# An eleventh weight slot, a moved scatter, split last loads and a shared last norm in a two-layer mixture-of-experts trunk

## The chip, the core and the metric

The kernel runs on one core of one Trainium2 chip. The core has a matrix engine (TensorE, in the profile PE, its weight loads PEld), a vector engine (VectorE, DVE), an activation engine (ScalarE, ACT), GpSimd (POOL) and SyncE (SP), which here does nothing but start DMA transfers from memory into SBUF. The metric is the device time of one execution in microseconds (us), lower is better.

## What is computed

256 latent tokens and 256 context tokens of width 1024 pass through two layers. Layer 0 mixes tokens by differential attention, layer 1 by pooling over windows of 2, 4, 8 and 16 tokens. Behind each mixer comes a norm, then a mixture of 16 experts with two chosen for each token, then a second norm:

```python
def expert_block(args):
    xb, e = args
    return (jax.nn.silu(xb @ wg[e]) * (xb @ wu[e])) @ wd[e]
...
y2 = moe_ffn(tokens, router_w, router_b, moe_wg[i], moe_wu[i], moe_wd[i])
xl = deepnorm_update(xl, y2[:B * S].reshape(B, S, D), g2, ln_g[i, 1], ln_b[i, 1])
```

`deepnorm_update` is `layer_norm(ALPHA * x + (1 + gate) * y, g, b)`. The gates and shifts come from a product of the condition vector with `mod_w`, two times 1024 x 6144. Everything is float32. `wg`, `wu` and `wd` of one expert are three matrices of 1024 x 1024, 12.6 MB together, and all 32 experts are read once: 403 of the 480 MB that the program moves.

## The kernel before

The code is written out by hand for each engine, and semaphores tie the engines together. An engine works strictly through its own list.

**The ring.** Expert weights stream through `ring`, ten slots of 2 MB (128 partitions x 4096 floats). A unit is half a matrix, so an expert has six: 0 and 1 are `wg`, 2 and 3 `wu`, 4 and 5 `wd`. Unit number v counts through both layers; the small weights of the pooling mixer are a unit of their own between them (number 96), so the last unit is 192. SyncE sends unit v into slot `FREE[v % RING]` once TensorE has signalled `unit_used` for unit v - RING. The first ten units have conditions of their own in `slot_free`, since the slots still hold attention weights, q, k and v, or partial results then. The loads stand in one queue and land in order.

**The early part.** VectorE computes the condition products: 20 units of `mod_w` (here "sum units", in `LOADS` the bare numbers) come as halves of 1 MB into slots 2 and 3 by turns, and eight multiply-adds each sum them up (L1309), between the softmax steps of the attention. `LOADS` is the order in which SyncE sends all these.

**An expert.** At most 64 tokens per expert take part in the main path (a loop for further tokens, `further_experts`, follows each layer and is not entered with these inputs). TensorE multiplies the gathered tokens with the four units of `wg` and `wu` into PSUM banks 4 and 5 (`two_halves`, L887), gathers tokens of a coming pair of experts into bank 6 (`gather`, L879), waits until ScalarE and VectorE have made silu(a) * b (`h_ready`), turns that result (`turn_hidden`, L903), turns the routing weights of the next expert (L909), waits for the turned result to be copied to SBUF (`hTt_copied`, L1647), multiplies it with the two units of `wd` into bank 6, waits for VectorE to scale that with the gate into `ysb` (`ys_ready`, L1651), and adds it to the tokens' sums in banks 0 to 3 (`scatter`, L895). Banks 0 to 3 hold token tile t, half h in bank 2t + h until the layer ends.

**Small jobs.** `job` on TensorE and `job_out` on VectorE spread gates and other rows over partitions, one behind each of experts 1 to 6 of layer 0 (`LATE_JOB`). The last norm's gain rows are spread in layer 1's last two experts (`last_row`, L926) and copied by ScalarE into `joint`; its shift rows are spread behind the last scatter into banks 4 and 5.

**The last norm** (`last_norm`). VectorE waits for the whole last scatter and reads the count of further rounds. Then it takes statistics of the four banks (L1478), combines them for each tile (L1474), and makes two passes over each of the four 128 x 512 pieces: subtract the mean and multiply with the gain (L1537), then divide by the deviation and add the shift from PSUM (L1543). ScalarE makes only the two square roots. SyncE stores each piece when `out_ready` counts it.

## Time and profile before

| quantity | value |
|---|---|
| median of 3 runs (lowest, highest) | 1221.16 us (1218.96, 1221.24) |
| the profiled execution's own time | 1220.21 us |
| its span, first to last instruction | 1218.4 us |
| TensorE busy | 1130.0 us, 93% |
| VectorE, ScalarE, GpSimd busy | 357.8, 166.8, 5.2 us |
| moved by DMA | 480.17 MB, mean 394 GB/s |
| mean granted TensorE clock | 0.987 |

The profile is one execution. [...] A row of the timeline joins like instructions that follow each other, x64 for 64 of them; each product counts twice here, since a float32 product runs as two instructions. Idle time in front of an instruction stands in brackets, with what ended it. "DMA to landing" is the time from a transfer's issue to its arrival.

### The profile page before, as it was taken

To read this page: it belongs to the slowest core of one execution; us is meant where nothing else is said; L and a number is where in the kernel's file an instruction comes from. 1 tells how busy PE (TensorE), PEld (TensorE's weight loads), DVE (VectorE), ACT (ScalarE), POOL (GpSimd) and SP (SyncE) were. 2 spreads that over 40 slices of the span, in tenths; PEclk is the share of its full clock that TensorE was granted. 3 is DMA by queue.
4 is the path that set the end of the run, shared out by engine and by line. 5 is a ranking of instruction groups with operands and counts; after the bars stand their busy time and mean duration, and the time that the engine had idled before them with its cause. 6 is when DMAs were issued, how large, how long until landed. Compare 5 with 4: busy or idle time off the path is not lost.

```text
span 1218.4 us, 12360 instructions
## 1 busy us (share of the span) xinstructions
PE 1130.0 (93%) x5288; PEld 500.6 (41%) x5288; DVE 357.8 (29%) x729; ACT 166.8 (14%) x398; POOL 5.2 (0%) x8
## 2 busy tenths in 40 slices
PE   8998998899999999999999999999999999999995
PEld 3553554545344333333333337533333343333331
DVE  1559899763111211111111115211111111111113
ACT  1101233523000000000100006100000010000000
POOL 0000000000000000000000010000000000000000
PEclk9998999999999999999999999999999999999998
DMA  9998797984999999999999999899999999999993
GB/s 394 405 356 322 270 358 273 401 345 167 428 427 429 427 429 426 429 427 427 428 428 428 427 419 427 357 427 429 427 428 429 425 429 427 428 429 426 429 426 153
DMA packets 40153, 480.17 MB, mean 394 GB/s; under 512 B 5024, under 2 KB 6304, under 8 KB 8352
## 3 DMA queue, kind: packets, MB, share of 16 engines
q1 hardware_dynamic: 39040, 476.91, 93.9%
q10 hardware_dynamic: 1056, 2.43, 0.6%
q8 instruction: 44, 0.72, 0.2%
q14 instruction: 13, 0.11, 0.0%
HBM read 476.18 MB, written 1.05 MB: 392 GB/s over the span
## 4 chain that ended last, share of the span: by engine, by line
PE 82%; DVE 9%; DMA 6%; issue 2%; ACT 1%; DVEq 0%; ACTq 0%
PE ps L887 53%; PE ps L879 5%; PE ps L895 5%; DMA ring<-in_moe_wu 3%; PE ps L638 3%; DMA ring<-in_mod_w 3%; PE ps L738 2%; PE ps L641 2%; DVE work L1647 2%; DVE work L1651 1%; DVE ring L1309 1%; PE ps L903 1%; PE ps L579 1%; PE ps L701 1%; PE ps L644 1%
## 5 line engine op out<-in xcount | busy, mean ns | idle before, releaser
L887 PE MATMUL ps<-ring,tra 128*64 128x512 f32 x2048 | 446.7, 594 | 1.0 <-DMA ring<-in_moe_wu 1.0
L887 PEld LDWEIGHTS ps<-ring,tra 128*64 128x64 f32 x2048 | 144.1, 137 | 298.4 <-issue 295.7
L887 PE MATMUL ps<-ring,work 128*64 128x512 f32 x1024 | 228.7, 598 | 29.2 <-DVE work L1647 29.2
L887 PEld LDWEIGHTS ps<-ring,work 128*64 128x64 f32 x1024 | 83.2, 137 | 154.1 <-issue 117.3
L1642 DVE TENSOR_TENSOR work<-ps,work 128x512 f32<-128x512 f32 x32 | 22.1, 692 | 277.2 <-ACT work L1198 277.2
L1198 ACT ACTIVATE work<-ps 128x512 f32<-128x512 f32 x32 | 19.1, 597 | 533.5 <-PE ps L887 533.5
L895 PE MATMUL ps<-work,extra 64*128 64x512 f32 x256 | 63.6, 615 | 21.0 <-DVE work L1651 21.0
L1191 ACT ACTIVATE tra<-ps,cols 128x128 f32<-128x128 f32 x128 | 48.1, 456 | 240.2 <-PE ps L879 240.2
L1645 DVE TENSOR_TENSOR work<-work,ps 128x512 f32<-128x512 f32 x32 | 22.0, 689 | 181.7 <-PE ps L887 181.7
L879 PEld LDWEIGHTS ps<-extra,xn 128*128 128x128 f32 x512 | 61.0, 195 | 24.3 <-issue 22.7
L879 PE MATMUL ps<-extra,xn 128*128 128x128 f32 x512 | 66.9, 285 | 1.4 <-DVE extra L1555 1.4
L638 PE MATMUL ps<-ring 128*128 128x512 f32 x128 | 58.5, 612 | 0.7 <-ACT ring L1073 0.7
L895 PEld LDWEIGHTS ps<-work,extra 64*128 64x128 f32 x256 | 22.0, 186 | 61.4 <-DVE work L1651 46.3
L1651 DVE TENSOR_TENSOR work<-ps,gt 128x512 f32<-128x512 f32 x16 | 11.1, 691 | 116.9 <-PE ps L887 116.9
L1651 DVE TENSOR_TENSOR work<-ps,rows 128x512 f32<-128x512 f32 x16 | 11.1, 691 | 115.5 <-PE ps L887 115.5
L1309 DVE SCALAR_TENSOR_TENSOR ring<-ring,cols 128x512 f32<-128x512 f32 x56 | 42.1, 752 | 3.2 <-DMA ring<-in_mod_w 1.2
L638 PEld LDWEIGHTS ps<-ring 128*128 128x128 f32 x128 | 24.5, 196 | 33.9 <-issue 33.8
L1647 DVE COPY work<-ps 128x512 f32<-128x512 f32 x32 | 22.2, 692 | 50.0 <-PE ps L903 50.0
L1309 DVE SCALAR_TENSOR_TENSOR extra<-ring,cols,extra 128x512 f32<-128x512 f32 x42 | 31.6, 752 | 2.2 <-DMA ring<-in_mod_w 0.7
L1309 DVE SCALAR_TENSOR_TENSOR modp<-ring,cols,modp 128x512 f32<-128x512 f32 x42 | 31.6, 752 | 1.5
L579 PE MATMUL ps<-cst 128*128 128x512 f32 x44 | 24.6, 691 | 4.2 <-DMA cst<-in_consts 4.0
L644 PE MATMUL ps<-ring 128*128 128x256 f32 x128 | 28.4, 380 | 0.0
(184 smaller groups left out, 712.4 us busy)
## 6 DMA issues: line engine op xcount, KB each, us to landing
ring<-in_moe_wg SPq DMA_DIRECT2D x64, 2048.0 KB, 23.9
ring<-in_moe_wu SPq DMA_DIRECT2D x64, 2048.0 KB, 23.4
ring<-in_moe_wd SPq DMA_DIRECT2D x64, 2048.0 KB, 23.0
ring<-in_mod_w SPq DMA_DIRECT2D x40, 1024.0 KB, 9.7
ring<-in_mod_w SPq DMA_DIRECT2D x4, 2048.0 KB, 18.5
ring<-in_attn_wqkv SPq DMA_DIRECT2D x4, 2048.0 KB, 11.2
ring<-in_attn_wo SPq DMA_DIRECT2D x2, 2048.0 KB, 10.9
ring<-in_tokens SPq DMA_DIRECT2D x2, 1024.0 KB, 16.3
```

Source lines behind the costliest of these rows:

```text
L579: mm(bank(bk), ident, cst[:, 0:NB], start=True, stop=True, skip_group_check=True)
L638: return mm(bank(acc_bank(g)), w[:, k, t * P:t * P + P], hT[:, k, :], start=first, stop=end)
L641: return mm(bank(acc_bank(g)), hT[:, k, t * P:t * P + P], rhs, start=first, stop=end)
L644: last = mm(bank(acc_bank(g), 0, P, n * TOK, (n + 1) * TOK), w[:, k, hd * P:hd * P + P], hT[:, k, 0:TOK], start=first and n == 0, stop=end ...
L738: last = mm(bank(2 * t + h), oT[t][:, k, :], wo[:, k, :], start=(k == 0), stop=(k == KT - 1))
L879: last = mm(bank(bk, 0, P, k * P, k * P + slots), xn[:, c0:c0 + P], sgat[:, t, 0:slots], start=(t == 0), stop=(t == TT - 1), skip_group_ch ...
L887: last = mm(ps[SLOTS * h:SLOTS * h + SLOTS, b, :], lhs(k0 + k), w[:, k, h * NB:(h + 1) * NB], start=(k0 + k == 0), stop=(k0 + k == KT - 1) ...
L895: last = mm(bank(2 * t + h), sw[SLOTS * h:SLOTS * h + SLOTS, t * P:t * P + P], ysb[SLOTS * h:SLOTS * h + SLOTS, :], start=False, stop=True ...
L1191: nc.scalar.activation(xg[i // 2 % 2][:, kk, :], bank(bk, k * P, k * P + P), ACT.Identity, bias=one(bcol[2 * layer], kk, 1), scale=one(aco ...
L1309: ins = v_.scalar_tensor_tensor(out=acc, in0=w[:, k, :], scalar=ck, in1=acc, op0=ALU.mult, op1=ALU.add)
L1647: v_.tensor_copy(work[:, NB:2 * NB], bank(7)).then_inc(sem("hTt_copied"), 1)
L1651: v_.tensor_tensor(ysb, bank(6), gt[layer], ALU.mult).then_inc(sem("ys_ready"), 1)
```

## The change

Four edits, named here in the order of the program.

1. The ring has eleven slots (`RING = 11`). The room in SBUF comes from a smaller scratch area for DMA descriptors that GpSimd would write, which this program doesn't use (`dynamic_dma_scratch_size=128`). Slot 10 is new and first in `FREE`. `AHEAD = 1`: unit 0 of layer 0 goes there without a condition, in the list `LOADS` behind sum unit 9. All other early units keep their slot and condition under a number higher by one.
2. TensorE's scatter of expert e no longer stands behind its down product but in the next expert, behind the turning of its hidden result. The last expert of each layer keeps a scatter of its own at the end.
3. Units 3 and 5 of the very last expert are sent as two loads of 1 MB with a semaphore each (`LAST_UNITS`, `last_unit`), and TensorE multiplies each half when it is there.
4. The last norm: gain and shift rows are spread as jobs behind experts 1 to 4 of layer 1 and copied to SBUF by VectorE (`joint`, `lnb`); the last scatter signals each bank (`summed`), and VectorE starts its statistics bank by bank; piece (tile 0, half 1) is made by ScalarE (subtract and divide) and GpSimd (multiply, add), and the stores go in another order.

```diff
-RING = 10
-FREE = (4, 8, 5, 9, 6, 7, 2, 3, 1, 0)
+RING = 11
+FREE = (10, 4, 8, 5, 9, 6, 7, 2, 3, 1, 0)
+LAST_UNITS = tuple(LAYER_BASE[1] + (NE - 1) * EU + n for n in (3, 5))
...
-LATE_JOB = {e: EARLY_JOBS + e - 1 for e in range(1, 7)}
+LATE_JOB = {(0, e): EARLY_JOBS + e - 1 for e in range(1, 7)} | {(1, e): EARLY_JOBS + 5 + e for e in range(1, 5)}
...
+                if v in LAST_UNITS:
+                    load(to[:, 0:2], of[:, 0:2], sem(f"last_first_{n}"))
+                    load(to[:, 2:4], of[:, 2:4], sem(f"ring_loaded_{s}"))
+                else:
+                    load(to, of, sem(f"ring_loaded_{s}"))
...
+            z = xn[:, NB:D]
+            pool.wait_ge(sem("job_out"), len(JOBS))
+            pool.wait_ge(sem("last_scaled"), 1)
+            nc.gpsimd.tensor_tensor(z, z, joint[:, NB:D], ALU.mult).then_inc(sem("last_weighed"), 1)
+            pool.wait_ge(sem("last_weighed"), 1)
+            nc.gpsimd.tensor_tensor(z, z, lnb[1], ALU.add).then_inc(sem("pool_out"), 1)
...
+            def last_unit(b, lhs, v, n, k0):
+
+                w = slot(ring_slot(v)[0]).rearrange("p (k n) -> p k n", k=4)
+                pe.wait_ge(sem(f"last_first_{n}"), 16)
+                two_halves(b, lhs, w, k0, range(2))
+                landed(pe, v)
+                return two_halves(b, lhs, w, k0, range(2, 4))
...
+                if e:
+                    pe.wait_ge(sem("ys_ready"), q)
                 if pr_ + 1 < PAIRS:
                     pe.wait_ge(sem("sgat_ready"), PAIRS * layer + pr_ + 2)
                     gather(6, e2).then_inc(sem("gather_done"), 1)
...
                 turn_hidden().then_inc(sem("hT_turned"), 1)
+                if e:
+                    scatter(swT[(e - 1) % 2]).then_inc(sem("scattered"), 1)
...
-                pe.wait_ge(sem("ys_ready"), q + 1)
-                scatter(swT[e % 2]).then_inc(sem("scattered"), 1)
+                if q == DEPTH * NE - 1:
+                    pe.wait_ge(sem("ys_ready"), q + 1)
+                    scatter(swT[e % 2], sem("summed")).then_inc(sem("summed"), 1)
+                elif e == NE - 1:
+                    pe.wait_ge(sem("ys_ready"), q + 1)
+                    scatter(swT[e % 2]).then_inc(sem("scattered"), 1)
...
             std(3, 0)
+            act.wait_ge(sem("last_shift"), 1)
+            nc.scalar.activation(xn[:, NB:D], bank(1), ACT.Identity, bias=mv[:, 4:5], scale=mv[:, 2:3])\
+                .then_inc(sem("last_scaled"), 1)
             std(3, 1)
...
+                dve.wait_ge(sem("job_out"), len(JOBS))
+                for h in range(2):
+                    half_stats(0, h)
+                spread(n, 0)
+                half_stats(1, 0)
+                dve.wait_ge(sem("std_ready"), TT * n + 1)
+                link(v_.reciprocal(mv[:, 2:3], mv[:, 3:4]))
+                v_.scalar_tensor_tensor(out=mv[:, 4:5], in0=mv[:, 0:1], scalar=-1.0, in1=mv[:, 2:3], op0=ALU.mult,
+                                        op1=ALU.mult).then_inc(sem("last_shift"), 1)
+                half_stats(1, 1)
+                spread(n, 1)
+                weighed(0, 0)
+                dve.wait_ge(sem("var_ready"), TT * n + 2)
+                for h in range(2):
+                    weighed(1, h)
```

SyncE's list in the early part, before, from sum unit 9 (the second row of `in_mod_w` begins with it) to the first expert units (`in_moe_wg`):

```order
L418 DMA ring<-in_attn_wqkv 128x4096 [waits unit_used]
L418 DMA ring<-in_mod_w 128x2048 [waits half_summed] x8
L418 DMA ring<-in_attn_wqkv 128x4096 [waits unit_used]
L418 DMA ring<-in_mod_w 128x2048 [waits half_summed] x4
L418 DMA ring<-in_attn_wo 128x4096 [waits unit_used]
L418 DMA ring<-in_mod_w 128x2048 [waits half_summed] x6
L418 DMA ring<-in_attn_wo 128x4096 [waits unit_used]
L418 DMA xn<-in_x 128x2x1024
L418 DMA ring<-in_mod_w 128x2048 [waits half_summed] x4
L418 DMA ring<-in_moe_wg 128x4096 [waits unit_used]
```

And now:

```order
L422 DMA ring<-in_mod_w 128x2048 [waits half_summed] x2
L422 DMA ring<-in_moe_wg 128x4096
L422 DMA ring<-in_mod_w 128x2048 [waits half_summed] x6
L422 DMA ring<-in_attn_wqkv 128x4096 [waits unit_used]
L422 DMA ring<-in_mod_w 128x2048 [waits half_summed] x4
L422 DMA ring<-in_attn_wo 128x4096 [waits unit_used]
L422 DMA ring<-in_mod_w 128x2048 [waits half_summed] x6
L422 DMA ring<-in_attn_wo 128x4096 [waits unit_used]
L422 DMA xn<-in_x 128x2x1024
L422 DMA ring<-in_mod_w 128x2048 [waits half_summed] x4
L422 DMA ring<-in_moe_wg 128x4096 [waits unit_used]
```

The load of 2 MB without a wait stands behind the two halves of sum unit 9; the six halves of units 10 to 12 follow it, and the first unit with a condition (`unit_used`) stands where unit 0 stood.

TensorE in layer 1, an expert with an even number, from the turning of the next weights to the next expert's first unit (`ring_loaded_` and a slot number), before:

```order
L909 MATMUL ps<-cst,extra 128x128 [waits ssc_ready]
L909 MATMUL ps<-cst,extra 128x128
L887 MATMUL ps<-ring,work 64x512 [waits ring_loaded_0,xg_copied,hTt_copied]
L887 MATMUL ps<-ring,work 64x512 x7
L887 MATMUL ps<-ring,work 64x512 [waits ring_loaded_4]
L887 MATMUL ps<-ring,work 64x512 x7
L895 MATMUL ps<-work,extra 128x512 [waits ys_ready]
L895 MATMUL ps<-work,extra 128x512 x3
L887 MATMUL ps<-ring,tra 64x512 [waits ring_loaded_8,swT_copied,xg_copied]
```

And now, from the gather of such an expert on (`L931` is the turning, `L921` the scatter):

```order
L905 MATMUL ps<-extra,xn 128x128 [waits sgat_ready,ys_ready]
L905 MATMUL ps<-extra,xn 128x128 x7
L931 MATMUL ps<-cst,work 128x128 [waits h_ready]
L931 MATMUL ps<-cst,work 128x128 x3
L921 MATMUL ps<-work,extra 128x512 x4
L937 MATMUL ps<-cst,extra 128x128 [waits ssc_ready]
L937 MATMUL ps<-cst,extra 128x128
L913 MATMUL ps<-ring,work 64x512 [waits ring_loaded_5,xg_copied,hTt_copied]
L913 MATMUL ps<-ring,work 64x512 x7
L913 MATMUL ps<-ring,work 64x512 [waits ring_loaded_9]
L913 MATMUL ps<-ring,work 64x512 x7
L913 MATMUL ps<-ring,tra 64x512 [waits ring_loaded_6,swT_copied,xg_copied]
```

The scatter has lost its wait for `ys_ready` (the gather, which writes the same bank, has it), and stands between the turning and the down product that waits for `hTt_copied`; the next expert's first unit stands directly behind the down product.

VectorE in the last norm, before:

```order
L1478 BN_STATS stat<-ps 128x6
L1478 BN_STATS stat<-ps 128x6 [waits dve_chain]
L1474 BN_AGGR mv<-stat 128x2 [waits dve_chain]
L1478 BN_STATS stat<-ps 128x6
L1478 BN_STATS stat<-ps 128x6 [waits dve_chain]
L1474 BN_AGGR mv<-stat 128x2 [waits dve_chain]
L1537 SCALAR_TENSOR_TENSOR xn<-ps,mv,modp 128x512 [waits lng_copied,var_ready]
L1541 RECIPROCAL mv<-mv 128x1 [waits std_ready,dve_chain]
L1543 SCALAR_TENSOR_TENSOR xn<-xn,mv,ps 128x512 [waits lnb_spread,dve_chain]
```

And now:

```order
L1521 BN_STATS stat<-ps 128x6 [waits summed,job_out]
L1521 BN_STATS stat<-ps 128x6 [waits summed,dve_chain]
L1517 BN_AGGR mv<-stat 128x2 [waits dve_chain]
L1521 BN_STATS stat<-ps 128x6 [waits summed]
L1590 RECIPROCAL mv<-mv 128x1 [waits std_ready,dve_chain]
L1591 SCALAR_TENSOR_TENSOR mv<-mv 128x1 [waits dve_chain]
L1521 BN_STATS stat<-ps 128x6 [waits summed]
L1517 BN_AGGR mv<-stat 128x2 [waits dve_chain]
L1576 SCALAR_TENSOR_TENSOR xn<-ps,mv,modp 128x512
L1581 SCALAR_TENSOR_TENSOR xn<-xn,mv,pscale 128x512 [waits dve_chain]
```

Each statistic waits for its own bank's sum, two small instructions for ScalarE's share stand between them, and the second pass reads its shift from `pscale` in SBUF where it read `ps`.

## Rows read from the trace of the kernel before

**Rows 1.** Windows of core 0: stretch, length, busy by engine, PEclk, DMA share, GB/s

```profile
275.00:291.00 16.00, 14.65 (x112) 10.99 (x106) 8.01 (x41) 9.01 (x20) 0.00 (x0) 0.98 0.00 0
292.00:765.00 473.00, 444.98 (x2230) 192.50 (x2227) 85.57 (x215) 51.21 (x108) 4.96 (x4) 1.00 1.01 426
765.00:775.00 10.00, 10.00 (x54) 5.80 (x55) 1.68 (x7) 3.01 (x8) 0.00 (x0) 0.89 0.57 212
```

**Rows 2.** Timeline of the end: start, length, engine, line, count, idle before and releaser

```profile
1184.65 0.42 PEld L887 LDWEIGHTS ps<-ring,tra 128*64 128x64 f32 x4 [0.44 <-DMA ring<-in_moe_wu]
...
1189.55 0.20 PEld L887 LDWEIGHTS ps<-ring,tra 128*64 128x64 f32 x4 [1.91 <-DMA ring<-in_moe_wu]
...
1195.60 7.34 PE L887 MATMUL ps<-ring,work 128*64 128x512 f32 x32 [0.79 <-DVE work L1647]
...
1199.29 0.20 PEld L887 LDWEIGHTS ps<-ring,work 128*64 128x64 f32 x4 [0.92 <-DMA ring<-in_moe_wd]
...
1203.74 1.99 PE L895 MATMUL ps<-work,extra 64*128 64x512 f32 x8 [0.80 <-DVE work L1651]
...
1206.63 1.43 DVE L1478 BATCH_NORM_STATS2 stat<-ps 128x6 f32<-128x512 f32 x2 [2.95 <-PE ps L895]
...
1215.24 0.75 DVE L1543 SCALAR_TENSOR_TENSOR xn<-xn,mv,ps 128x512 f32<-128x512 f32 x1
```

**Rows 3.** TensorE timeline, first units of two successive experts in layer 1

```profile
1124.48 13.95 PE L887 MATMUL ps<-ring,tra 128*64 128x512 f32 x64
...
1151.85 0.65 PE L887 MATMUL ps<-ring,tra 128*64 128x512 f32 x2
```

**Rows 4.** Single ring loads on SyncE: issue time, and time from issue to landing

```profile
L418 SPq DMA_DIRECT2D ring<-in_moe_wd x1: 328/328/328, 680.3 to 680.3; - x1
DMA to landing us min/median/max: 37.6/37.6/37.6
...
L418 SPq DMA_DIRECT2D ring<-in_moe_wu x1: 328/328/328, 748.0 to 748.0; - x1
DMA to landing us min/median/max: 24.4/24.4/24.4
...
L418 SPq DMA_DIRECT2D ring<-in_moe_wd x1: 328/328/328, 772.4 to 772.4; - x1
DMA to landing us min/median/max: 7.9/7.9/7.9
```

**Rows 5.** Timeline and windows, last expert of layer 0, and one window later

```profile
714.17 0.74 PE L903 MATMUL ps<-cst,work 128*128 128x128 f32 x4 [0.86 <-DVE work L1645]
...
715.70 8.78 PE L887 MATMUL ps<-ring,work 128*64 128x512 f32 x32 [0.79 <-DVE work L1647]
...
724.53 0.69 DVE L1651 TENSOR_TENSOR work<-ps,gt 128x512 f32<-128x512 f32 x1 [8.89 <-PE ps L887]
...
716.10:719.50 3.40, 3.40 (x10) 0.98 (x8) 0.00 (x0) 0.00 (x0) 0.00 (x0) 0.50 1.06 383
...
1187.10:1190.50 3.40, 2.37 (x14) 0.64 (x12) 0.00 (x0) 0.00 (x0) 0.00 (x0) 1.00 1.00 419
```

**Rows 6.** Second half of sum unit 9 on SyncE, and VectorE at unit 10

```profile
L418 SPq DMA_DIRECT2D ring<-in_mod_w x1: 328/328/328, 109.5 to 109.5; - x1
DMA to landing us min/median/max: 8.8/8.8/8.8
...
127.58 0.48 DVE L1307 TENSOR_SCALAR modp<-ring,cols 128x512 f32<-128x512 f32 x1
```

**Rows 7.** Waits of TensorE: who waited for whom: us in total, times, longest

```profile
PE ps L887 <- DVE work L1647: 29.2, 32, 0.9
...
PE ps L895 <- DVE work L1651: 21.0, 27, 0.8
```

**Rows 8.** Groups of instructions: ScalarE from PSUM, and GpSimd's products

```profile
L1198 ACT ACTIVATE work<-ps 128x512 f32<-128x512 f32 x32 | 19.1, 597 | 533.5 <-PE ps L887 533.5
...
L541 POOL TENSOR_TENSOR ring<-ring,modp 128x512 f32<-128x512 f32 x4 | 5.0, 1270 | 720.5 <-DMA ring<-in_pool_w 720.5
```

More of the change, by code:

```diff
@@ L469, in _ @@
                     load_rows()
+                elif what == "ahead":
+                    for n in range(AHEAD):
+                        load_unit(0, 0, n)
                 elif what == "x":
@@ L768, in job @@
                     last = columns_of(bk, rows[1], 1, NMOD, 4 * NMOD)
+                elif kind in ("lng", "lnb"):
+                    last = mm(bank(bk), pick((10 if kind == "lng" else 18) + int(n)), rows[0][:, :], start=True, stop=True)
                 elif kind == "joint":
@@ L889, in two_halves, with scatter @@
                 return last
-            def scatter(sw):
+            def scatter(sw, each=None):
                 for t in range(TT):
@@ L896, in scatter @@
                                   ysb[SLOTS * h:SLOTS * h + SLOTS, :], start=False, stop=True, skip_group_check=True)
+                        if each is not None and (t, h) != (TT - 1, 1):
+                            last.then_inc(each, 1)
                 return last
@@ L1682, in body @@
                     v_.tensor_tensor(ysb, bank(6), gt[layer], ALU.mult).then_inc(sem(x_ + "ys"), 1)
[L1683 to L1684 removed]
+                scattered = lambda: dve.wait_ge(*((sem("scattered"), NE) if layer == 0 else (sem("summed"), 2 * TT)))
+                if layer == 0:
+                    scattered()
+                further(dve, layer, chunk, body, first=scattered if layer else None,
+                        end=lambda: dve.wait_ge(sem("further_done"), layer + 1))
             def pool_layer():
```

153 lines of the change are left out of this document (75 added, 78 removed).

## The prediction

> **What bounds the kernel now.** I read the shares of the page first: TensorE is busy 93% of the span, and the core moves 394 GB/s on average. The windows say where the rest of the stream is. Between 275 and 291 us the queues move nothing, from 292 to 765 they run at 426 GB/s, and from 765 to 775 there is a second hole [rows 1]. The reader is to see two machines: TensorE, which looks busy, and the weight stream, which from 292 us on stops nowhere else.
>
> Which of the two ends last? One expert is 12.6 MB in six units. Where TensorE waits for loads, units come 4.90 us apart (1189.55 - 1184.65) [rows 2], so the stream needs 29.4 us for an expert. TensorE starts an expert every 27.37 us (1151.85 - 1124.48) [rows 3]. TensorE is the faster one and eats up the lead that a full ring gives the stream, 2.0 us per expert. In layer 0 the lead just suffices: the last unit lands at 680.3 + 37.6 = 717.9 [rows 4], and TensorE, which has begun the last two units at 715.70, doesn't wait for it [rows 5]. In layer 1 it doesn't suffice: the last units are waited for, the last until 1199.29, and from there to the end of the span it is 19.1 us [rows 2]. The end of the kernel is thus the end of the weight stream plus a tail.
>
> **The ring and the early load.** What fills a hole in the stream brings all later loads forward; bytes stay the same. The first hole arises because all ten slots are full at 275 and the first is released at 291. Every old unit keeps its condition, shifted by one number, and the new unit 0 goes to slot 10, which nobody uses earlier. So at 291 one unit more is on board and every later unit lands one place, 4.90 us, earlier. This is paid where unit 0 is sent, behind sum unit 9: that half is issued at 109.5 and lands at 118.3 (109.5 + 8.8) [rows 6]. With 4.9 us more the queue is at 123.2, the first half of sum unit 10 (1 MB, half of 4.9) lands at about 125.7, and VectorE takes it at 127.58 [rows 6]. So it costs nothing, with 1.9 us to spare; if the cover were gone, VectorE's sums, and with them all that follows, would be up to 4.9 us late.
>
> The second hole: the load issued at 748.0 lands at 772.4 (24.4), the next is issued only at 772.4, when the first unit of layer 1 has been multiplied, and lands 7.9 us later [rows 4]. Units follow at 4.9 otherwise, so 3.0 us are lost. After the change one more unit may be loaded before this release, and the stream is one unit ahead: the queue is busy until the same 772.4. The release itself comes earlier (next part, by 7.2 us, at 765.2); issued 7.2 us before the queue ends, the load has no hole before it. Gain 3.0. The last unit then lands at 1199.3 - 4.9 - 3.0 = 1191.4.
>
> **The scatter behind the next turning.** TensorE's wait for the scaled result before each scatter (21.0 us in 27 waits, 0.78 each) and its wait for the copied turning (29.2 in 32, 0.91 each) are both covered now [rows 7]; by the single rows they are 0.8 and 0.95, so an expert falls from 27.37 to about 25.6 us. I cost this at nearly nothing although it is 16 x 1.7 = 28 us per layer. Left to itself TensorE would end layer 0 some 26 us before 724.5, at about 698, but the last unit lands only at 717.9 - 4.9 = 713.0. What hides the gain is the stream. It shows only at the two layer ends. In layer 0 before, the last pair of units ran from 715.70 to 724.53 [rows 5]. Now the end is set by unit 3 of expert 15, which lands at 713.0 - 9.8 = 703.2: 3.65 for its products (a quarter of the 13.95 of four units [rows 3], and 0.15 to their end), 0.9 to the turning, and from the turning's start to the down product 1.5 (715.70 - 714.17) [rows 5] plus 0.9, since the scatter (1.99, of which the old wait covers about 1.1) stands there now, then twice the products, 7.1. That gives 717.3, 7.2 earlier. All of the layer boundary moves with it.
>
> **The tail.** In layer 1 the units 3 and 5 of the last expert come as two halves. Unit 2 lands at 1191.4 - 14.7 = 1176.7 and takes 3.65; unit 3, half of it early, ends at 1183.9; 0.9 to the turning, 2.4 to the down product, 7.1 for it: 1194.3, which is 2.9 after the last landing, against 3.7 before (1202.94 - 1199.29) [rows 2]. From there 0.8 to the scatter, as before (1203.74 - 1202.94).
>
> From the scatter's start to VectorE's last end it was 1215.99 - 1203.74 = 12.25 [rows 2]. VectorE began 2.9 after the scatter's start and can now begin after a quarter of it, about 0.7: -2.2. Two of its eight passes of 0.75, at 0.71 apart, go to ScalarE and GpSimd: -1.4. Two [128x1] instructions more in the chain: +0.1. The spreading products leave TensorE's end, where nobody waited long for them. So 8.75. The side branch: ScalarE (0.60) and twice GpSimd (1.27 each) [rows 8] from about 3.5 give 6.9, before VectorE's end, so its store is no bound. The stores' own 2.4 stay.
>
> **Sum.** The last landing -7.9, products behind it -0.8, norm -3.5: 12.2 off the span of 1218.4, so 1206.2, and with the 1.8 that lie around it in the profiled execution (1220.2) 1208.0. The median of the runs is 0.95 above that execution, 1221.2, so by the median it would be 1209.0; I say 1208.3. Bounds: the ring between 4.9 and 0 (early load in the way); second hole 3.0 to 0; scatter's added time in the last expert 0 to 1.99; VectorE's start 0.5 to 1.0 after the scatter's; the GpSimd branch 1.27 to 2 x 1.27 per pass, the longer one giving 9.4 and 0.7 more. The four loads of 1 MB in place of two of 2 MB: nothing to 0.4 us more; I take nothing, since no row sets the two sizes apart.
>
> **GpSimd beside VectorE.** No row shows a VectorE instruction with both inputs in SBUF beside a GpSimd instruction. The nearest is the scaling at 724.53, with one input in PSUM, which ran 0.69 beside GpSimd's four [rows 5, 8], the mean of its kind; so the sum above takes 0, and the bound is that each of two passes waits out one GpSimd pass, 2 x 1.27. [...]
>
> **Rivals.**
> [...]
> - *The early load is in the way*: sum unit 10 late, all later by up to 4.9: 1213.2. Against it the 1.9 us of margin.
> - *The boundary doesn't come earlier* (a wait in layer 0's last expert that I don't see): the hole of 3.0 stays in part: 1211.
> - *The loads don't move, only the tail does*: 1221.2 - 4.3 = 1216.9. It needs a stream that slows when more units are outstanding; but the load that took 37.6 us to land [rows 4] stood behind seven others at 4.9 each.
> [...]
> - *TensorE is the bound after all*: 32 x 1.7 = 54 faster, 1167. It needs loads closer than 4.90; no row has them.
>
> **How the numbers follow.** Forecast (both holes filled, shorter tail, no lock) 0.46, with the lock 0.30, early load in the way 0.08, boundary 0.05, tail alone 0.06, slower clock 0.04, TensorE bound 0.01. Within 0.2% (2.4 us, about what a measurement of this kernel can tell from none) lies half of the tail-alone case. Faster 0.93, same 0.03, slower 0.04. The range from 1205.2 (no scatter in the last turning, VectorE starting at 0.5, and 1 us as two executions differ) to 1212.2 (lock and one slow stretch at the end, or part of a hole left) holds the first two cases and most of the fourth.
>
> **What the profile after would show.** No unit's landing later than one unit earlier from 300 on; windows without a hole at 765 to 775 and with 11 to 12 us of nothing in place of 16 before 291; waits of TensorE for loads in the last third of each layer, no waits for the scaled result; first statistics 0.7 after the last scatter's start, not 2.9. Wrong would be: sum unit 10 waited for, GpSimd's second pass ending behind VectorE's last, a clock of 0.50 in many windows, or units further apart than 4.9.

## The result and the profile after

The changed kernel takes 1204.05 us (median of 4 runs, 1203.59 to 1207.20), the kernel before beside it 1220.06 us (median of 4, 1218.74 to 1221.24). The ratio is 0.9865, with a 95% interval from 0.9847 to 0.9882: 16.0 us less, where 12.2 were forecast as a sum. The profiled execution took 1203.59 us with a span of 1201.6, against 1220.21 and 1218.4, so its span is 16.8 us shorter.

The page of the changed kernel: busy times with shares of the span, and the chain that ended last.

```profile
span 1201.6 us, 12396 instructions
...
PE 1134.2 (94%) x5288; PEld 494.0 (41%) x5288; DVE 362.4 (30%) x732; ACT 166.6 (14%) x397; POOL 8.0 (1%) x10
...
PE 69%; DMA 23%; DVE 6%; ACT 1%; issue 1%; another core or an unknown queue 0%; DVEq 0%; SPq 0%; ACTq 0%
```

TensorE is no less busy than before. 23% of the chain is now waiting for DMA.

The windows that answer to [rows 1], with one ahead of the first hole and one at the end (columns as there, times in us from the span's start; PEclk is the granted clock as a share of TensorE's full speed):

```profile
208.00:276.00 68.00, 60.42 (x256) 33.02 (x260) 46.04 (x91) 27.83 (x74) 0.00 (x0) 0.91 0.89 361
276.00:292.00 16.00, 14.67 (x110) 11.01 (x104) 8.01 (x41) 9.02 (x20) 0.00 (x0) 0.96 0.00 0
292.00:760.00 468.00, 450.35 (x2254) 192.03 (x2250) 87.29 (x216) 52.78 (x112) 4.94 (x4) 0.99 1.01 428
...
765.00:775.00 10.00, 10.00 (x50) 3.57 (x47) 1.20 (x2) 0.60 (x1) 0.00 (x0) 1.00 1.01 418
...
775.00:1180.00 405.00, 388.68 (x1877) 150.16 (x1877) 61.93 (x133) 31.54 (x73) 0.00 (x0) 1.00 1.01 430
```

Three things are to be seen. The second hole is gone (418 GB/s from 765 to 775, against 212). The first hole is as long as it was, 16 us of nothing. And the stream runs faster between the holes: 428 where it was 426, though both stretches hold slower pieces. An undisturbed stretch of both kernels shows it better. First before, then after:

```profile
800.00:1150.00 350.00, 327.51 (x1616) 132.62 (x1612) 50.37 (x114) 27.31 (x65) 0.00 (x0) 1.00 1.01 427
```

```profile
800.00:1150.00 350.00, 338.90 (x1638) 129.86 (x1636) 54.06 (x118) 27.36 (x65) 0.00 (x0) 1.00 1.01 431
```

That is 0.9% more bytes in the same time. By the landings of single units in the trace, the median step from one 2 MB unit to the next fell from 4.894 to 4.848 us. Of the packets of 16 KB, 29% took 611 ns before, with a median of 613 and 13% at 620 or more; now 97% take 611. Between 800 and 1150 the mean packet took 616.0 ns before and takes 612.2 now.

The single loads that answer to [rows 4, 6] (issue time, then the time to landing):

```profile
L422 SPq DMA_DIRECT2D ring<-in_moe_wg x1: 433/433/433, 109.9 to 109.9; - x1
...
DMA to landing us min/median/max: 14.4/14.4/14.4
...
L422 SPq DMA_DIRECT2D ring<-in_moe_wd x1: 328/328/328, 292.1 to 292.1; - x1
...
DMA to landing us min/median/max: 8.7/8.7/8.7
...
L422 SPq DMA_DIRECT2D ring<-in_moe_wd x1: 328/328/328, 764.1 to 764.1; - x1
...
DMA to landing us min/median/max: 10.2/10.2/10.2
...
L422 SPq DMA_DIRECT2D ring<-in_moe_wd x1: 4215/4215/4215, 1145.6 to 1145.6; - x1
...
DMA to landing us min/median/max: 40.2/40.2/40.2
```

The early load lands at 124.3 and is in nobody's way. The load released at 764.1 has to queue (10.2 us, where 7.9 was a load without a queue). The last unit lands at 1145.6 + 40.2 = 1185.8, 13.45 earlier than the 1199.25 of before.

The timeline of the tail, which answers to [rows 2]:

```profile
1166.13 3.65 PE L913 MATMUL ps<-ring,tra 128*64 128x512 f32 x16 [1.12 <-DMA ring<-in_moe_wg]
...
1171.00 7.09 PE L913 MATMUL ps<-ring,tra 128*64 128x512 f32 x32 [1.21 <-DMA ring<-in_moe_wu]
...
1181.61 7.09 PE L913 MATMUL ps<-ring,work 128*64 128x512 f32 x32
...
1188.74 0.69 DVE L1705 TENSOR_TENSOR work<-ps,rows 128x512 f32<-128x512 f32 x1 [8.25 <-PE ps L913]
...
1189.49 1.99 PE L921 MATMUL ps<-work,extra 64*128 64x512 f32 x8 [0.79 <-DVE work L1705]
...
1190.72 1.43 DVE L1521 BATCH_NORM_STATS2 stat<-ps 128x6 f32<-128x512 f32 x2 [1.28 <-PE ps L921]
...
1194.12 0.70 DVE L1576 SCALAR_TENSOR_TENSOR xn<-ps,mv,modp 128x512 f32<-128x512 f32 x1
...
1194.30 1.26 POOL L563 TENSOR_TENSOR xn<-xn,modp 128x512 f32<-128x512 f32 x1 [475.42 <-ACT xn L1285]
1194.85 1.27 DVE L1581 SCALAR_TENSOR_TENSOR xn<-xn,mv,pscale 128x512 f32<-128x512 f32 x1
1195.64 1.59 POOL L565 TENSOR_TENSOR xn<-xn,gt 128x512 f32<-128x512 f32 x1
...
1198.48 0.75 DVE L1581 SCALAR_TENSOR_TENSOR xn<-xn,mv,gt 128x512 f32<-128x512 f32 x1
```

The down product ends at 1188.70, 2.9 behind the last landing (3.7 before). VectorE starts 1.23 after the scatter and ends at 1199.23, 9.74 after the scatter's start (12.25 before). One second pass takes 1.27 in place of 0.75, beside GpSimd.

So the span's 16.8 us are 13.45 at the last landing, 0.8 in the products and 2.5 in the norm. If the forecast's two terms hold, the landing's part is one unit (4.85) and the second hole (3.0), less 1.0, since the stream restarts later after the first hole in this execution (the load lands at 300.74 and not at 299.71); the 6.6 that remain would be the pace, for which the forecast had no term. The experiments measure each of the three. What remained to be found out was whether the pace belongs to the program, and which edit brought it.

### The profile page after: what moved, and what is told of

The parts are those of the page before. It is cut to its first block, busy times and chain, and to the rows that moved or that the text cites. A ratio compares the mean times of both kernels' runs of the same rounds, so it can differ in the third digit from the quotient of the medians.

```text
span 1201.6 us, 12396 instructions
## 1 busy us (share of the span) xinstructions
PE 1134.2 (94%) x5288; PEld 494.0 (41%) x5288; DVE 362.4 (30%) x732; ACT 166.6 (14%) x397; POOL 8.0 (1%) x10
## 4 chain that ended last, share of the span: by engine, by line
PE 69%; DMA 23%; DVE 6%; ACT 1%; issue 1%; another core or an unknown queue 0%; DVEq 0%; SPq 0%; ACTq 0%
PE ps L913 41%; DMA ring<-in_moe_wu 12%; DMA ring<-in_moe_wg 8%; PE ps L905 4%; PE ps L921 4%; DMA ring<-in_mod_w 3%; PE ps L662 3%; PE ps L762 2%; PE ps L665 2%; DVE ring L1350 1%; PE ps L725 1%; PE ps L668 1%; PE ps L743 1%; DVE modp L1350 1%; PE ps L578 1%; PE ps L931 1%
## 5 line engine op out<-in xcount | busy, mean ns | idle before, releaser
L913 PE MATMUL ps<-ring,tra 128*64 128x512 f32 x2048 | 454.1, 597 | 24.2 <-DMA ring<-in_moe_wu 19.2
L913 PEld LDWEIGHTS ps<-ring,tra 128*64 128x64 f32 x2048 | 147.5, 138 | 322.6 <-issue 280.8
L913 PEld LDWEIGHTS ps<-ring,work 128*64 128x64 f32 x1024 | 71.6, 137 | 135.6 <-issue 133.3
L921 PE MATMUL ps<-work,extra 64*128 64x512 f32 x256 | 63.6, 615 | 1.6 <-DVE work L1705 1.6
L921 PEld LDWEIGHTS ps<-work,extra 64*128 64x128 f32 x256 | 22.0, 186 | 22.1 <-issue 15.1
L1684 DVE COPY extra<-ps 128x256 f32<-128x256 f32 x32 | 13.6, 424 | 48.4 <-PE ps L937 48.4
```

What stands on the lines that cost most here:

```text
L913: last = mm(ps[SLOTS * h:SLOTS * h + SLOTS, b, :], lhs(k0 + k), w[:, k, h * NB:(h + 1) * NB], start=(k0 + k == 0), stop=(k0 + k == KT - 1) ...
L921: last = mm(bank(2 * t + h), sw[SLOTS * h:SLOTS * h + SLOTS, t * P:t * P + P], ysb[SLOTS * h:SLOTS * h + SLOTS, :], start=False, stop=True ...
```

## The experiments

In each, "before" is the kernel before on the same chip. The first four take the ring and the pace apart.

**1. The kernel before, unchanged, once more.**

> The kernel before, unchanged, on the chip on which the next three run. In the two profiles at hand a unit of 2 MB took 4.895 us in the kernel before and 4.845 in the changed one, already for the loads before 100 us that both send alike. If this pace belongs to the chip or the day, this run has the same pace as the changed kernel on this chip. If it belongs to the program (where its slots lie in SBUF, or the room kept for descriptors), it stays at 4.90 here and the changed kernel at 4.85. Time: equal to itself, within 0.2%.

Measured: 1220.03 us against 1220.56, ratio 0.9997 (0.9987 to 1.0006); units 4.895 us apart. So the pace is no matter of the chip or of the moment.

**2. The small scratch alone.** The change also reserves 128 bytes for the DMA scratch in place of the default 16 KB, to make room for the eleventh slot.

```diff
-    nc = bacc.Bacc("TRN2", target_bir_lowering=False, num_devices=1)
+    nc = bacc.Bacc("TRN2", target_bir_lowering=False, num_devices=1, dynamic_dma_scratch_size=128)
```

> Before, with only the scratch for descriptors cut from 16 KB to 128 bytes for each partition, so that every tile lies some 16 KB lower. If the place in SBUF or the scratch sets the pace of the loads, units land 4.85 apart here against 4.90 in the run beside it, and the end comes 1 to 2.5 us earlier, which is what TensorE waits for loads at the end of layer 1. If not, no change: 0 us, pace as in the run beside it.

Measured: 1217.78 us against 1220.56, ratio 0.9974 (0.9965 to 0.9983). Units come 4.848 us apart and the last lands at 1196.25, 3.0 earlier; TensorE waits for no load at all, and its down product ends only 1.5 earlier, at 1201.46. 97% of the 16 KB packets take 611 ns. This one edit brings the pace. Its down product follows VectorE's copy and no load:

```profile
1194.38 7.09 PE L887 MATMUL ps<-ring,work 128*64 128x512 f32 x32 [0.78 <-DVE work L1647]
```

**3. The ring and the early load, with the small scratch.**

```diff
-RING = 10
-FREE = (4, 8, 5, 9, 6, 7, 2, 3, 1, 0)
+RING = 11
+FREE = (10, 4, 8, 5, 9, 6, 7, 2, 3, 1, 0)
...
+LOADS = [... ("q", 1), 9, "ahead", 10, 11, 12, ("v", 1), 13, 14,
...
+AHEAD = 1
...
+    nc = bacc.Bacc("TRN2", target_bir_lowering=False, num_devices=1, dynamic_dma_scratch_size=128)
```

> Before, with the eleventh slot and the early load of unit 0 and the small scratch, the rest as it was. Mine: the stream is one unit (4.9 us) ahead, but TensorE is then the bound at 27.37 us per expert through both layers; only its waits for loads in the last expert go, 1.5 to 2.5 us faster. The rival, that loads moved forward pay by themselves, gives 5 to 8 us faster. If the early load were in the way of sum unit 10, the start of the experts (287.5) would be up to 5 us later and the time not better.

Measured: 1218.34 us against 1220.56, ratio 0.9981 (0.9972 to 0.9990): no better than the scratch alone. The last unit lands another 1.7 earlier (1194.55) although this profile's experts began 3.4 later than in the kernel before, at 290.9, after stretches of a lower granted clock (0.80 from 276 to 291, against 1.00); nobody profits, because TensorE, without a wait for a load, needs until 1204.78.

**4. The changed kernel once more.**

> The changed kernel, unchanged, on the same chip as the first three: again some 16 us faster than the kernel before. Its pace of loads beside that of the first run tells whether the 5.6 us that my sum lacked up to the last landing come from the program or from the chip: with equal paces the gap to the kernel before would be 11 to 12 us here, with 4.90 against 4.85 it stays at 16.

Measured: 1204.80 us, ratio 0.9870 (0.9855 to 0.9885), units 4.855 apart, last landing 1186.39.

The next two take the scatter.

**5. The moved scatter alone.**

```diff
+                if e:
+                    pe.wait_ge(sem("ys_ready"), q)
...
                 turn_hidden().then_inc(sem("hT_turned"), 1)
+                if e:
+                    scatter(swT[(e - 1) % 2]).then_inc(sem("scattered"), 1)
...
-                pe.wait_ge(sem("ys_ready"), q + 1)
-                scatter(swT[e % 2]).then_inc(sem("scattered"), 1)
+                if e == NE - 1:
+                    pe.wait_ge(sem("ys_ready"), q + 1)
+                    scatter(swT[e % 2]).then_inc(sem("scattered"), 1)
```

> Before, with only the scatter moved behind the next expert's turning (ten slots, full scratch). Mine: each expert of TensorE falls from 27.37 to about 25.6 us where units are there, but the stream ends where it did, so layer 0 ends 2 us earlier, the second hole shrinks by that much, and the kernel is 1.5 to 2.5 us faster. The rival, that TensorE's saved waits count (32 x 1.7), gives up to 54 us faster.

Measured: 1219.0 us against 1220.94, ratio 0.9992 (0.9983 to 1.0001), so between nothing and 2 us. In the profile layer 0 ends 1.6 earlier (722.9), the second hole closes (4.90 us between the two landings there, where it was 7.88) and the last landing is 2.5 earlier (1196.78), at 4.896 a unit; TensorE now waits 42.5 us for loads, where it waited 1.0.

**6. The changed kernel with the scatter in its old place.** The diff is the reverse of the last, but the very last scatter keeps its signal for each bank.

> The changed kernel with the scatter back in its old place, all else kept (eleven slots, halves, last norm, small scratch). If ring and scatter pay only together, this is TensorE at 27.37 us per expert through both layers and the time is that of the ring alone less about 2.6 for the last norm, 1215.5 to 1216.5, so that undoing the scatter costs 11 us. If the parts add up, it costs only the 2 us of the run with the scatter alone, 1206.5.

Measured: 1216.21 us against 1220.94, ratio 0.9962 (0.9949 to 0.9976). Undoing an edit that is worth 1 to 2 us alone costs 11 to 12. Its timeline at the end and its window at the second hole:

```profile
1194.96 0.69 DVE L1697 COPY work<-ps 128x512 f32<-128x512 f32 x1 [0.84 <-PE ps L931]
1195.71 7.09 PE L913 MATMUL ps<-ring,work 128*64 128x512 f32 x32 [0.78 <-DVE work L1697]
...
765.00:775.00 10.00, 10.00 (x54) 6.17 (x55) 1.68 (x7) 3.01 (x8) 0.00 (x0) 0.85 0.26 88
```

The last unit has landed at 1191.97, but the down product starts at 1195.71, released by VectorE's copy and by no load: TensorE is the bound. The faster stream only makes the second hole deeper (88 GB/s where it was 212), since TensorE frees the next slot at 773 as ever. From the first expert of layer 1 to its down product's end TensorE takes 433.5 us here without a wait for a load (769.3 to 1202.8). The kernel before took 434.2 (768.7 to 1202.95). So before the change the two bounds stood close together at the end, 1.5 us apart by the profile of experiment 2. Speeding up one alone gave 2.8 us by the medians (2.1 to 4.3) for the stream and 1.9 (0 to 2.1) for TensorE, with the eleventh slot on top of the quick stream nothing more; both together give the 16.

The next seven say what sets the pace. Each was executed once and agrees with the kernel before in its time to within what single executions differ by, so what counts is the pace in its trace and not its time.

**7. The small scratch with every tile at its old address.**

```diff
+        sb("pad", 4064)
         ring = sb("ring", RING * UNIT)
...
+    nc = bacc.Bacc("TRN2", target_bir_lowering=False, num_devices=1, dynamic_dma_scratch_size=128)
```

> Before, with the scratch of 128 bytes and a dead tile of 16256 bytes in front of the ring, so that every tile lies where it lies in the kernel before. If the place of the tiles sets the pace, units land 4.895 us apart as in the kernel before; if the scratch does, 4.848 as in the run with the small scratch. Time 1218 to 1221 either way.

Measured: 1223.79 us in one run (its experts began at 291.2 and not at 287.5, so 3.7 us of it are the early part), units 4.895 apart, and 29% of the 16 KB packets took 611 ns, as in the kernel before. The same scratch with the tiles moved gave 4.848 and 97% (experiment 2). It isn't the scratch, it is where the tiles lie.

Where is that? My expectations give every address 128 too low. The ring is the kernel's first tile, but ahead of it stand the scratch and 128 bytes of constants that the allocation itself puts there: its next free byte before the first tile is 16481 with the default scratch and 225 with the small one, and a tile begins at the next multiple of 32. So the ring begins at byte 16512 of each partition with the default scratch, and at byte 256 with the small one; in this experiment the unused tile of 16256 bytes begins at 256, and the ring at 16512 as in the kernel before. The sizes agree: with 256 unused bytes ahead of the ring and the default scratch, the allocation has reached byte 229344 before the last small tile, which is 16384 + 128 + 256 and 212576 for the tiles between. The titles below have the true addresses.

**8. The default scratch, and 128 unused bytes ahead of the ring,** which puts it at byte 16640.

```diff
+        sb("pad", 32)
         ring = sb("ring", RING * UNIT)
```

> The kernel before with an unused tile of 128 bytes per partition ahead of the ring, default scratch: the ring begins at byte 16512 of a partition and not at 16384 (with the small scratch it begins at 128). Theory A (what counts is where a slot begins within some power of two, and 128 bytes off is what the changed kernel has): loads every 4.848 us, nearly all 16 KB packets 611 ns, time 1216.5 to 1219. Theory B (what counts is the absolute place, the lower 16 KB being the quicker, or the total distance of 16 KB): loads every 4.895 us, packets spread from 611 to 622 ns, time 1219 to 1224.

Measured: 1218.89 us in one run, units 4.853 apart, 97% of the 16 KB packets at 611 ns. So 128 bytes are enough. The window of an undisturbed stretch:

```profile
800.00:1150.00 350.00, 327.66 (x1614) 132.54 (x1610) 50.09 (x113) 27.31 (x65) 0.00 (x0) 1.00 1.01 431
```

**9. The ring at byte 16576.** As the last, with `sb("pad", 16)`.

> The kernel before with an unused tile of 64 bytes ahead of the ring, which then begins at byte 16448 of a partition (257 x 64). Theory A (only a ring on a multiple of 16 KB is slow): loads every 4.85 us, packets 611 ns. Theory B (a multiple of 128 bytes that is not one of 16 KB is what is quick, and 64 off is not enough or costs more): 4.89 or longer, packets above 611 ns. Time 1216 to 1220 under A.

Measured: 1219.77 us in one run, units 4.894 apart; only 14% of the 16 KB packets took 611 ns, 46% 613 and 19% 620. Theory A fell; B stood until experiments 10, 11 and 13.

**10. The ring at byte 2176.** Small scratch and `sb("pad", 480)`.

> The kernel before with the 128-byte scratch and an unused tile of 1920 bytes: the ring begins at byte 2048. Theory A (only multiples of 16 KB are slow): loads every 4.85 us. Theory C (any multiple of 2 KB or more is slow): every 4.89 us, packets from 611 to 622 ns.

Measured: 1222.88 us in one run (experts from 290 on), units 4.893 apart. The pace is the one that Theory C gives, but at 2176 the ring is on no multiple of 2 KB, so its reason falls too.

```profile
800.00:1150.00 350.00, 328.29 (x1620) 132.98 (x1618) 49.56 (x112) 27.31 (x65) 0.00 (x0) 1.00 1.01 428
```

**11. The ring at byte 8320.** Small scratch and `sb("pad", 2016)`.

> The kernel before with the 128-byte scratch and an unused tile of 8064 bytes: the ring begins at byte 8192. Theory A (only multiples of 16 KB are slow): loads every 4.85 us. Theory C (a large power of two is slow): every 4.89 us. If 2048 is quick and 8192 slow, the bound lies between.

Measured: 1220.09 us in one run, units 4.895 apart. As in the last, the pace of Theory C without its reason.

**12. The ring at byte 16512 as before, all other tiles 128 bytes on.** `sb("pad", 32)` behind the ring.

> The kernel before with an unused tile of 128 bytes behind the ring, default scratch: the ring stays at byte 16384, every other tile lies 128 bytes further on. Theory (what counts is the address that a load writes to, so the ring): expert units every 4.89 us, 16 KB packets from 611 to 622 ns, time 1219 to 1224. Rival (it is the place of the tiles that the engines work in, beside which the loads write): 4.85 us, 611 ns, 1217 to 1219.

Measured: 1220.75 us in one run, units 4.894 apart, 30% of the packets at 611 ns. Moving the other tiles by these 128 bytes does nothing; moving the ring with them (experiment 8) does all.

**13. The ring at byte 384.** Small scratch and `sb("pad", 32)`.

> The kernel before with the 128-byte scratch and an unused tile of 128 bytes ahead of the ring: the ring begins at byte 256 of a partition. Theory A (odd multiples of 128 bytes are quick, even ones slow): expert units every 4.89 us, packets from 611 to 622 ns, time 1219 to 1224. Theory B (any small multiple of 128 bytes past a multiple of 2 KB is quick): 4.85 us, 611 ns, time 1216 to 1219.

Measured: 1219.63 us in one run, units 4.895 apart.

```profile
800.00:1150.00 350.00, 327.53 (x1614) 132.64 (x1612) 50.77 (x115) 27.34 (x65) 0.00 (x0) 1.00 1.01 428
```

Theory A foresaw the pace, but with 128 added to each address its rule turns round. Of the seven places tried, 256 and 16640, both multiples of 256, are quick; 384, 2176, 8320 and 16512, odd multiples of 128, and 16576, an odd multiple of 64, are slow. Slots are 16 KB per partition, so all of them share the ring's offset. All seven fit one rule: a slot that begins on a multiple of 256 bytes is quick. Two quick places are few, both are odd multiples of 256, and a ring at byte 512 was not run. An eighth place, byte 16768 (256 unused bytes, default scratch), has no result: the tiles don't fit in SBUF any more.

The next three undo parts of the change in the kernel in which the stream is the bound.

**14. The changed kernel with ten slots and without the early load,** small scratch kept.

```diff
-RING = 11
-FREE = (10, 4, 8, 5, 9, 6, 7, 2, 3, 1, 0)
+RING = 10
+FREE = (4, 8, 5, 9, 6, 7, 2, 3, 1, 0)
...
-AHEAD = 1
+AHEAD = 0
...
```

The conditions in `slot_free` go back by one number with it.

> The changed kernel with ten ring slots again and without the early load; the 128-byte scratch stays. Theory (the stream bounds, and the forecast's ring terms of 4.9 and 3.0 were right): 2 MB loads land every 4.85 us as in the changed kernel, the last one near 1193.7 (1185.8 + 7.9), and the time is 1212.3 (1211.5 to 1213.5). Rival 1 (the pace comes with the eleventh slot): loads every 4.895, last landing near 1200, time about 1218.5. Rival 2 (the ring gives nothing once the scatter is moved, as it gave nothing to the kernel before beyond the small scratch): time within 1.5 us of 1204.5.

Measured: 1209.08 us against 1220.24, ratio 0.9913 (0.9896 to 0.9929). Last landing 1190.78. The slot is worth 5.0 us, and not the 7.9 that I expected: of the second hole only a rest comes back with ten slots, so it was the moved scatter that had filled most of it.

```profile
765.00:775.00 10.00, 10.00 (x48) 3.30 (x46) 0.69 (x1) 0.60 (x1) 0.00 (x0) 1.00 0.92 365
```

The rest is 1.3 us: at 774.6 a unit lands 6.18 after the one before it, where a step is 4.85. At the quick pace the stream reaches this place earlier, so its hole is larger than before: in experiment 2 the same step is 11.61.

**15. As the last, and the default scratch too.**

> As the run above, and the scratch back at its default, so that every tile is at its old address: what is left of the change is the moved scatter, the halved last units and the last norm. Theory (place of the tiles): loads every 4.895 us, last landing near 1200 (1193.7 + 6.6), time 1218.7 less the small part that layer ends absorb, so 1217.5 to 1219.5. Rival (the small scratch is worth only the 2.5 us that it gave to the kernel before): 1214.5 to 1215.5. The tail behind the last landing should be 3.3 us shorter than before in either (1.6 is the forecast's 0.8 + 2.55 for the norm by the changed kernel's trace).

Measured: 1215.29 us against 1220.24, ratio 0.9964 (0.9950 to 0.9978); units 4.896 apart, last landing 1196.59. The place of the ring is worth 6.2 us here (1215.29 to 1209.08; 5.8 by the last landings), against 2.8 in the kernel before. My expectation of 1217.5 to 1219.5 was too high, because it brought back a hole that the scatter fills. The rival's range is met, but not for its reason: it put the place at 2.5 on top of a slot of 7.9. The tail behind the last landing is 16.0 us, 3.1 shorter than before, where 3.3 were expected.

**16. The changed kernel, eleven slots, unit 0 sent behind the sum units.**

```diff
-LOADS = [... ("q", 1), 9, "ahead", 10, 11, 12, ("v", 1), 13, 14,
+LOADS = [... ("q", 1), 9, 10, 11, 12, ("v", 1), 13, 14,
...
-AHEAD = 1
+AHEAD = 0
...
-                if v < AHEAD:
+                if v == 0:
                     return
```

> The changed kernel with eleven slots, but the first expert unit sent after the sum units and not ahead of sum unit 10. Theory (one unit fetched early is one unit step less at the end): last landing near 1190.6 (1185.8 + 4.85), time 1209.3 (1208.3 to 1210.3). Rival (the early load pushed the restart of the stream back by 1.0, which comes back when it is gone): last landing 1189.6, time 1208.3. Rival 2 (the stretch in which it was sent was free of consequence because TensorE is late anyway): no change, 1204.5.

Measured: 1204.0 us against 1220.24, ratio 0.9872 (0.9855 to 0.9888), the same as the changed kernel; last landing 1184.34. The early load gives nothing. Its window where the first units are loaded:

```profile
208.00:276.00 68.00, 59.35 (x260) 31.77 (x260) 46.23 (x92) 28.24 (x76) 0.00 (x0) 0.95 0.94 394
276.00:291.00 15.00, 14.24 (x100) 11.03 (x102) 8.00 (x41) 8.51 (x19) 0.00 (x0) 1.00 0.00 0
```

Between 208 and 276 the changed kernel moved 361 GB/s, since loads there wait for slots that the attention still holds. Unit 0, with its own slot, finds room in that stretch (394 GB/s), and eleven units are on board before the hole either way, the last of them at 274.1 here and at 276.0 in the changed kernel.

**17. VectorE reads the last norm's shift from PSUM again.**

```diff
+            for h in range(2):
+                mm(bank(4 + h), pick(18 + h), rows[0][:, :], start=True, stop=True).then_inc(sem("lnb_spread"), 1)
...
-                    v_.scalar_tensor_tensor(out=z, in0=z, scalar=m_[:, 2:3], in1=lnb[h], op0=ALU.mult,
+                    dve.wait_ge(sem("lnb_spread"), h + 1)
+                    v_.scalar_tensor_tensor(out=z, in0=z, scalar=m_[:, 2:3], in1=bank(4 + h), op0=ALU.mult,
```

> The changed kernel, but VectorE's second passes of the last norm take the shift row from PSUM banks 4 and 5, as before the change (TensorE spreads it again behind the last scatter), GpSimd's still from SBUF. If VectorE and GpSimd lock each other out when VectorE has two inputs in SBUF, the second pass of the first piece falls from 1.27 to 0.75 us, GpSimd's add from 1.59 to about 1.27, and the end comes about 1.0 us earlier. If the length came from something else, nothing changes.

Measured: 1203.34 us against 1220.94, ratio 0.9860 (0.9844 to 0.9875). Its timeline:

```profile
1188.82 1.99 PE L921 MATMUL ps<-work,extra 64*128 64x512 f32 x8 [0.79 <-DVE work L1708]
...
1193.63 1.27 POOL L563 TENSOR_TENSOR xn<-xn,modp 128x512 f32<-128x512 f32 x1 [475.63 <-ACT xn L1287]
1194.18 0.75 DVE L1584 SCALAR_TENSOR_TENSOR xn<-xn,mv,ps 128x512 f32<-128x512 f32 x1
...
1194.98 1.26 POOL L565 TENSOR_TENSOR xn<-xn,gt 128x512 f32<-128x512 f32 x1
...
1197.26 0.75 DVE L1584 SCALAR_TENSOR_TENSOR xn<-xn,mv,ps 128x512 f32<-128x512 f32 x1
```

The same pass, still beside GpSimd, takes 0.75 and not 1.27, which is also what the changed kernel's last pass takes with two inputs in SBUF when GpSimd is done (1198.48). GpSimd's second product takes 1.26 and not 1.59, and VectorE ends 9.19 after the scatter's start and not 9.74: reading the shift from SBUF costs 0.55 us. The median is 0.7 below the changed kernel's, which is less than these runs can tell for sure.

**18. Both: no early load, shift from PSUM.**

> The changed kernel without the early load (unit 0 is sent behind the sum units) and with the shift of the last norm read from PSUM by VectorE. Theory: both changes keep their single results, 0 from the first and about 0.6 to 1 us from the second, so 1203.3 (1202.5 to 1204.3), the same as the run with the PSUM shift alone. Rival (the early load delays the restart of the stream by up to 1 us, as the landings say): 1202.3.

Measured: 1203.32 us (5 runs, 1201.98 to 1206.01) against 1220.3, ratio 0.9861 (0.9842 to 0.9881). As the last; the early load can be left out. The rival falls: without the early load the stream restarts as late as in the changed kernel (first landing at 300.63). By the medians these two versions are the fastest that I ran.

**The edits in one row.** By medians: before 1220.2; the scatter alone 1219.0; with the tail too (experiment 15) 1215.3; with the ring at byte 256 (14) 1209.1; with the eleventh slot (16) 1204.0; with the early load, the changed kernel, 1204.05 to 1204.8. So 1 to 2, 3.7, 6.2, 5.1 and 0.

The same steps by the landings, from the first behind the first hole to the last, without the tail:

| kernel | first, last landing | between |
|---|---|---|
| before | 299.71, 1199.25 | 899.5 |
| scatter and tail (15) | 299.81, 1196.59 | 896.8 |
| and the ring at byte 256 (14) | 299.36, 1190.78 | 891.4 |
| and the eleventh slot (the changed kernel) | 300.74, 1185.80 | 885.1 |

The scatter brings 2.8; the place 5.4, which is a pace of 6.7 less the 1.3 of the hole that ten slots leave (experiment 2, whose stretch is 896.6 with a hole of 6.8, against 899.5 with one of 3.0, gives the same 6.7 for the pace); the slot 6.4, the unit of 4.85, this 1.3, and 0.2 left over. Together 14.5, less the later restart 13.45.

## Why the prediction missed

The direction and the mechanism were right, and the time came 4.3 us below the forecast and 1.15 below the range. The step that failed is the price of a unit: "Units follow at 4.9 otherwise", with "bytes stay the same", from which the last landing came forward by 4.9 and 3.0 only. The last-landing term was 7.9 and measured 13.45; 6.6 to 6.7 of it are the pace of 4.848 us (the table above), by experiments 2, 7, 8 and 12 an effect of where the ring lies. The line of the diff that makes the scratch small was in front of me, and I read it as making room and took its price for nothing. The rival "TensorE is the bound after all" has the sentence that closed this door: loads closer than 4.90, "no row has them". True of the rows, but the rows were all of one placement.

Point by point:

- **The stream is the bound.** Only just. Experiment 2 shows that TensorE, with all units there in time, would have ended only 1.5 us earlier in the kernel before, and experiment 6 that it then bounds. I had the sizes for this [rows 2, 3] and costed the moved scatter "at nearly nothing". In the sum it did no harm, since the change has both; as a statement on the edits it is wrong, for without the scatter some 12 of the 16 us are gone.
- **The slot.** 4.90 forecast, 5.0 to 5.1 measured (14, 16). By the landings it is 6.4, since it also fills the 1.3 of the second hole that the quick pace would leave. The early load, to which the forecast tied it, has no part in it, and the first hole did not shrink to 11 to 12 us: the further unit fits into the slack between 208 and 276.
- **The early load costs nothing.** Right, but without the margin: sum unit 10's halves landed at 126.68 and 129.10, 1.2 to 1.5 later, and VectorE went from the work before it into its sums (at 126.65) without idle time. The 1.9 us forecast between landing and use were none here, since the half landed 1.0 later than forecast and VectorE came 0.9 earlier, and 0.65 in experiment 4 (127.55 to 128.20).
- **The second hole.** 3.0 forecast, 2.5 to 2.7 by the landings of experiments 5 and 15, all of it from the scatter at the old pace. The release of layer 1's first unit was forecast at 765.2 and came at 764.1.
- **Layer 0's end.** 717.3 forecast, 716.2 measured: the pace again, less a stretch at clock 0.50 that began at 697.2.
- **The products behind the last landing.** 2.9 forecast, 2.9 measured.
- **The norm.** 8.75 forecast from the scatter's start, 9.74 measured. Half of the difference is VectorE's start: 1.23 after the scatter's and not 0.7. The rows had it: before, VectorE began 0.9 behind the end of the whole scatter (2.89 - 1.99, [rows 2]), so a quarter of the scatter (0.5) and this hand-over make 1.4; I had counted 0.2 for it. The other half is VectorE's second passes beside GpSimd. No run shows that the two engines lock each other out, as the forecast's case "with the lock" (0.30) has it. What they show is the length of single passes: with two SBUF inputs the first took 1.27 beside a GpSimd product, where 0.75 is the pass with GpSimd idle (1198.48), and the second 0.78; with one input from PSUM it took 0.75 beside a GpSimd product too (experiment 17). By its record GpSimd had 0.71 to go when the first began and 0.22 when the second did, and they were 0.52 and 0.03 longer, so neither by all of that. Spans of GpSimd are rough in a trace.
- **The slower clock.** It did not come. The forecast gave 0.04 to a TensorE that is slower than before with its waits for loads; no run shows this term. In the changed kernel TensorE waited for loads 24 us in all, up to 2.3 at a time, in the last four or five experts of each layer, and in these stretches there is one at a granted clock of 0.50 in each layer (from 697.2 and from 1113.6, 3.4 us each). In experiment 5, with 42.5 us of such waits, there is none in them (1.00 from 581 to 725 and from 980 to 1195). The upper end of the range had both terms, the lock and one slow stretch at the end; from 1117 to the end of the last scatter the changed kernel's clock was 1.00.

That the range was missed by little is no merit: two errors of 1.0 each, the norm and the later restart of this execution, stood against the 6.6.

What stays open: whether every multiple of 256 bytes is quick (a ring at byte 512 would tell), and why the packets take 611 ns at one place and up to 622 at another, which no row tells. The ring is both what the loads write and what TensorE reads, and no run separates the two; in the first 60 us, 94% of the 16 KB packets already take 611 ns in the changed kernel, against 60% before.

## What to carry to other kernels

When two machines end within a microsecond or two of each other, an edit to one of them is worth little more than that distance, and the two together are worth far more than the sum of both alone (here 2.8 and 1.9, and 16 with the shorter tail): read from the trace where each would end without the other before pricing either. A change of allocation, here a buffer that only made room, moves every tile behind it and is an edit of its own; in a stream-bound kernel, begin the load buffers on a multiple of 256 bytes, as the two quick places here do, and try a few offsets, with the addresses read from the allocation and not worked out from the sizes that one knows of. And ask of a load that is sent earlier whether the stretch in which it went before was full.

## What the runs showed of the hardware

The pace of a saturated weight stream depends on the byte at which its buffers begin in a partition of SBUF. At bytes 256 and 16640, units of 2 MB come 4.85 us apart (430 to 431 GB/s) and 97% of the packets of 16 KB take 611 ns; at 384, 2176, 8320, 16512 and 16576, 4.89 to 4.90 us (427 to 428 GB/s), and 14 to 30% of the packets take 611 ns, the others mostly 612 to 622. Of these seven places the quick ones are the multiples of 256. That is 0.9% of a unit, or 6.2 us of this kernel once the stream is its bound.

VectorE's 128 x 512 pass with two inputs in SBUF took 1.27 us beside a GpSimd product and 0.75 with GpSimd idle, and 0.75 beside GpSimd when one input came from PSUM. GpSimd's add took 1.59 us in the first case and 1.26 in the last.
